# Every large on-chip tile moved to a multiple of 128 bytes (a two-block transformer in float32, one core)

## The chip, the cores and the metric

One core of one Trainium2 chip runs the whole program. The metric is the device time of one execution in microseconds; a figure for a kernel is the median of its runs. TensorE is PE in the profile (its weight loads are PEld), VectorE is DVE, ScalarE is ACT, GpSimd is POOL, and SP issues most of the DMAs.

## The reference

512 tokens of 1024 features pass two blocks in float32.

```python
def reference(x, mem, ...):
    x = x + hybrid_mixer(rms_norm(x))          # stick-breaking attention, gMLP, short conv; 3 gated branches; w_out
    x = x + memory_cross_attention(rms_norm(x), mem)   # 256 memory tokens: wk, wq, wv, wo
    x = x + swiglu(rms_norm(x))                # hidden 2816
    x = rms_norm(x, final_g)
    x = x + _mixer(_rms(x))                    # forget-gate attention, mLSTM, HGRN2; w_out_2
    x = x + _conv_glu(_rms(x))                 # hidden 2816, 3-tap causal conv on the up projection
    return x
```

## The kernel before

**Products.** Activations lie transposed, features on the 128 partitions and 512 tokens along the free axis, in 2 KiB slices. Every dense product is split: an operand is kept as a high part H, rounded to float32r, and a low part L, the rest, so one product is three matmuls (`mm3`, L361): H by H, L by H, H by L. 277 weight chunks of 128x1024 come from HBM one after the other into the ring `raw` (5 slots). ACT writes `WH` from it and DVE writes `WL` (L1465), each with 3 slots. PE uses chunks in the order of `PLAN`. The order on each engine is written out by hand, interleaved by fixed lists (`weave`), and all waits are semaphores that the author set; no tile framework adds any.

**Which operand is where.** In `tile` (L370) the weights are stationary (128 columns) and the activation slice moves (512 columns, 256 for the memory tokens). In `moving` (L382) and for wv of the cross attention the weights move and the activation is stationary. The activation pairs are:

- `XH`, `XL`: the normed input of a projection. Used by q, k, v, zv, zu, conv, the gates of the three branches, wq_xa, both ffn_up, and all input projections of the second block.
- `ZH`, `ZL`: branch outputs (288 matmuls), the input of w_out (192) and of wo_xa (192).
- `MH`, `ML`: the normed memory. Moving in wk_xa (8 tiles of 8 products), stationary in wv_xa.
- `HH1`, `HL1`, `HH2`, `HL2`: the hidden layers of the two feed-forward nets, for ffn_down1 and ffn_down2 (176 products each).
- `YYH`, `YYL`: the input of w_out2.

In the profile a matmul is named by its moving operand first: `pst<-HH,WL` moves `HH` against stationary `WL`. `HH` stands for both HH1 and HH2.

**Where the tiles lie.** A tile takes the same byte range in every partition. They are stacked in the order of the calls of `sb`, each start rounded up to 32 bytes, from byte 16512 (129 times 128) on. A closed stack gives its range back, so that `ZH`, `HH1`, `HH2`, `av1` and `YYH` all begin at the same byte, and q, k, kx, MH and so on lie over HH and HL. X, XH, XL, raw, WH, WL, cm and msk have sizes that are multiples of 128. Then come `col` (1168 bytes), `rcol` (16) and `gg` (32), after which every start is 96 past a multiple of 128, up to tiles behind other odd ones (`tmpb` 0 past, `pb` and `sg` 64 past).

Of the kernel before, what the change touches and what calls it, by code (L numbers as in the profile page):

```python
# [13 lines left out]
P = 128  # L14
T = 512
# [24 lines left out]
NCOLS = _n  # L40
# [109 lines left out]
def program(nc, xT, memT, wst, cols, rows, wsp, cmat, cmask, outT):  # L150
    es = ExitStack()
    with es:
        def sb(name, shape, dt=F32, stack=es):
            return stack.enter_context(nc.sbuf_tensor(name, shape, dt))
# [7 lines left out]
        raw = sb("raw", [P, NRAW, CH * P])  # L162
        WH = sb("WH", [P, NHL, CH * P], F32R)
        WL = sb("WL", [P, NHL, CH * P], F32R)
        cm = sb("cm", [P, 5, P])
        ones, upper, ident, halves, norms = (cm[:, i, :] for i in range(5))
        msk = sb("msk", [P, 8, P], U8)
        col = sb("col", [P, NCOLS])
        rcol = sb("rcol", [P, 4])
        gg = sb("gg", [P, 8])  # L170
        misc = sb("misc", [P, 6, T])
        acc = sb("acc", [P, 2, T])
        r_bc = misc[:, 0, :]
        rr = r12 = misc[:, 1, :]
        sq = [misc[:, 1, :], misc[:, 2, :]]
# [9 lines left out]
        st = ExitStack()  # L185
# [3 lines left out]
        row3 = sb("row3", [P, 3, T], stack=st)  # L189
        wT = sb("wT", [P, 4, P], stack=st)  # L190
        u, vz = X[:, 0:4, :], X[:, 4:8, :]
        ypad = sb("ypad", [P, T + 2], stack=st)
        tmpb = sb("tmpb", [P, 2, T], stack=st)
        st8 = sb("st8", [P, 16], stack=st)
        pb = sb("pb", [P, 2, 2, T], stack=st)
        sg_ = sb("sg", [P, 2, 2, T], stack=st)
        st.close()
        kx = sb("kx", [P, 8, MEM], stack=st)
        vx = sb("vx", [P, 2, D], stack=st)
        qx = sb("qx", [P, 8, T], stack=st)  # L200
        s8 = sb("s8", [P, 4, 8], stack=st)
        mrb = sb("mrb", [P, 4, MEM], stack=st)
        mraw = qx[:, 0:4, :].rearrange("p a (b t) -> p (a b) t", t=MEM)
        MH = sb("MH", [P, 8, MEM], F32R, st)
        ML = sb("ML", [P, 8, MEM], F32R, st)
        S2 = sb("S2", [P, 4, 2, MEM], stack=st)
        PT = [misc[:, 4:6, :], misc[:, 2:4, :], acc[:, :, :], mrb[:, :, :].rearrange("p (a b) t -> p a (b t)", b=2)]
        st.close()
        sty.close()
# [125 lines left out]
        def pe_program():  # L335
# [12 lines left out]
            def chunk(name):  # L348
# [3 lines left out]
                pe.wait_ge(wl, i + 1)  # L352
                return WH[:, i % NHL, :], WL[:, i % NHL, :]

            def units(w):
                return w.rearrange("p (u c) -> p u c", c=P)

            def mm(out, lhs, rhs, start=True, stop=True):
                return nc.tensor.matmul(out, lhs, rhs, start=start, stop=stop)  # L359
# [227 lines left out]
            def cross(s):  # L587
                b0, S = 4 + s, S2[:, s]
                for i in range(2):
                    free(b0)  # L590
                    pe.wait_ge(qx_ok, 2 * s + 2)
                    pe.wait_ge(kx_ok, 8)
                    for e in range(2):
                        for dd in range(2):
                            tb = (2 * i + e) * P
                            ins = mm(ps[b0][:, e * MEM:(e + 1) * MEM], qx[:, 2 * s + dd, tb:tb + P], kx[:, 2 * s + dd, :], dd == 0, dd == 1)
                    ins.then_inc(x_pe[s], 1)
                    yield
                    hold[b0] = (x_act[s], 3 * i + 2)
                    yield  # L600
                    yield
                    pe.wait_ge(x_dve[s], 5 * i + 5)
                    free(b0)
                    for si in range(2):
                        for e in range(2):
                            o = (2 * si + e) * P
                            ins = nc.tensor.transpose(ps[b0][:, o:o + P], S[:, e, si * P:(si + 1) * P], ident)
                    ins.then_inc(x_pe[s], 1)
                    yield
                    hold[b0] = (x_act[s], 3 * i + 3)  # L610
                pe.wait_ge(vx_ok, 2 * (s // 2) + 2)
                for dd in range(2):
                    b = b0 if dd == 0 else 2
                    free(b)
                    pe.wait_ge(x_act[s], 6)
                    for si in range(2):
                        ins = mm(ps[b][:, :], vx[:, si, s * 256 + dd * P:s * 256 + (dd + 1) * P], PT[s][:, si, :], si == 0, si == 1)
                    ins.then_inc(x_pe[s], 1)
                    yield
                hold[b0] = (zl_ok, 8 + 2 * s + 1)  # L620
                hold[2] = (zl_ok, 8 + 2 * s + 2)
                yield
# [230 lines left out]
            for m, b in enumerate(w_out2):  # L853
                i = PLAN.index(("w_out2", m))
                h, l = units(WH[:, i % NHL, :]), units(WL[:, i % NHL, :])
                for x, k in enumerate(YY_ORDER[6:]):
# [10 lines left out]
        def act_program():  # L867
# [3 lines left out]
            def run(func, out, in_, **kw):  # L871
                return nc.scalar.activation(out, in_, func, **kw)  # L872
# [229 lines left out]
            def cross(s):  # L1102
                b0, S, m_ = 4 + s, S2[:, s], s8[:, s]
                pv = ps[b0][:, :].rearrange("p (e s) -> p e s", s=MEM)
                for i in range(2):
                    yield
                    table(LNEXP)
                    act.wait_ge(x_dve[s], 5 * i + 2)
                    if i:
                        act.wait_ge(x_pe[s], 2)  # L1110
                    for e in range(2):
                        run(ACT.Exp, S[:, e, :], pv[:, e, :], bias=m_[:, e:e + 1], accum_out=m_[:, 2 + e:3 + e]).then_inc(x_act[s], 1)
                    yield
                    yield
                    yield
                    act.wait_ge(x_pe[s], 2 * i + 2)
                    run(ACT.Copy, PT[s][:, :, i * 256:(i + 1) * 256], ps[b0][:, :].rearrange("p (a t) -> p a t", t=256)).then_inc(x_act[s], 1)
                yield
                yield
                act.wait_ge(mm_, DONE["w_out", 7])  # L1120
                for dd in range(2):
                    act.wait_ge(x_pe[s], 5 + dd)
                    run(ACT.Copy, ZH[:, 2 * s + dd, :], ps[b0 if dd == 0 else 2][:, :]).then_inc(zh_ok, 1)
                yield
# [323 lines left out]
        def dve_program():  # L1448
# [12 lines left out]
            def split():  # L1461
                i = at["split"]
                at["split"] += 1
                dve.wait_ge(wh, i + 1)
                vec.tensor_tensor(WL[:, i % NHL, :], raw[:, i % NRAW, :], WH[:, i % NHL, :].bitcast(F32), ALU.subtract).then_inc(wl, 1)  # L1465

# [242 lines left out]
            def cross(s):  # L1709
                S, m_ = S2[:, s], s8[:, s]  # L1710
                pv = ps[4 + s][:, :].rearrange("p (e s) -> p e s", s=MEM)
                for i in range(2):
                    yield
                    dve.wait_ge(x_pe[s], 2 * i + 1)
                    vec.tensor_reduce(m_[:, 0:2], pv, AX.X, ALU.max).then_inc(x_dve[s], 1)
                    dve.wait_ge(x_dve[s], 5 * i + 1)
                    vec.tensor_scalar(m_[:, 0:2], m_[:, 0:2], -1.0, None, ALU.mult).then_inc(x_dve[s], 1)
                    yield
                    dve.wait_ge(x_act[s], 3 * i + 2)
                    vec.reciprocal(m_[:, 4:6], m_[:, 2:4]).then_inc(x_dve[s], 1)  # L1720
                    dve.wait_ge(x_dve[s], 5 * i + 3)
                    for e in range(2):
                        vec.tensor_scalar(S[:, e, :], S[:, e, :], m_[:, 4 + e:5 + e], None, ALU.mult).then_inc(x_dve[s], 1)
                    yield
                    yield
                yield
                yield
                for dd in range(2):
                    dve.wait_ge(zh_ok, 8 + 2 * s + dd + 1)
                    lo(ZL[:, 2 * s + dd, :], ps[4 + s if dd == 0 else 2][:, :], ZH[:, 2 * s + dd, :]).then_inc(zl_ok, 1)  # L1730
                yield
# [736 lines left out]
```

## Time and profile before

| | |
|---|---|
| median of 3 runs | 1736.02 us (1735.88 to 1737.95) |
| the profiled execution, its own time | 1737.55 us |
| its span, first to last instruction | 1735.8 us |
| mean granted TensorE clock | 0.994 |
| PE, PEld busy | 1692.5 us (98%), 1343.8 us (77%) |
| DVE, ACT, POOL busy | 896.8 us (52%), 657.7 us (38%), 163.3 us (9%) |
| DMA | 164.28 MB, 95 GB/s on average |

The durations that the profile gives matmuls overlap, since they are pipelined: a 128x512 matmul of 0.39 us starts some 0.23 us after the one before. The pace of PE is therefore read from starts: last start less first start, over the number of starts between them. The granted clock of 1.00 is TensorE's higher level (2.4 GHz), 0.5 the lower one (1.2 GHz).

### The profile page before, as it was taken

What the parts mean: (1) busy time and instruction counts of PE and PEld (TensorE: products, weight loads), DVE (VectorE), ACT (ScalarE), POOL (GpSimd) and SP (SyncE); (2) the same over time, 40 slices, a digit from 0 to 9 for tenths busy, and PEclk for the clock granted to TensorE, in tenths of its full rate; (3) what the DMA queues carried; (4) which work ended last, traced back from release to release, by engine and by line L of the source; (5) the groups of instructions that cost most, each with busy time, mean ns of one, the idle gap of its engine ahead of it and who ended that gap; (6) DMA issues with size and microseconds to landing.
All of it is one profiled execution on the core that took longest, in us unless ns stands there. A gap on an engine that the chain in (4) does not pass through costs nothing.

```text
span 1735.8 us, 19182 instructions
## 1 busy us (share of the span) xinstructions
PE 1692.5 (98%) x7824; PEld 1343.8 (77%) x7824; DVE 896.8 (52%) x1184; ACT 657.7 (38%) x935; POOL 163.3 (9%) x170
## 2 busy tenths in 40 slices
PE   7999999999999899999999999999999999999999
PEld 6777777778788668888888887777765888888887
DVE  4336664455463444444443326967545577777321
ACT  4244333333442433222222325246565444444211
POOL 2000100111110002000000111322111200000000
PEclk9999999999999999999999999999999999999999
DMA  6222222222433222223233223321212322323321
GB/s 241 85 86 73 73 73 85 78 93 97 158 101 105 73 86 94 96 97 97 97 97 103 87 91 103 132 99 62 61 37 91 102 98 96 97 95 97 103 92 54
DMA packets 47303, 164.28 MB, mean 95 GB/s; under 512 B 5024, under 2 KB 5152, under 8 KB 46896
## 3 DMA queue, kind: packets, MB, share of 16 engines
q1 hardware_dynamic: 46032, 158.88, 27.5%
q0 software_dynamic: 896, 3.70, 0.7%
q8 instruction: 62, 1.02, 0.2%
q10 hardware_dynamic: 288, 0.48, 0.1%
q14 instruction: 25, 0.20, 0.0%
HBM read 158.81 MB, written 4.23 MB: 94 GB/s over the span
## 4 chain that ended last, share of the span: by engine, by line
PE 90%; DVE 4%; ACT 3%; issue 2%; DMA 1%; POOL 0%; SPq 0%; ACTq 0%; DVEq 0%; POOLq 0%
PE pst L359 89%; ACT WH L872 1%; ACT L877 1%; PE pst L519 0%; PE pst L753 0%; DVE WL L1465 0%; DMA raw<-wst 0%; DMA X<-xT 0%; DVE qx L1684 0%; ACT ZH L872 0%; DVE XL L1477 0%; DVE ZL L1473 0%; DVE scr L2044 0%; ACT misc L872 0%; ACT Sx L872 0%
## 5 line engine op out<-in xcount | busy, mean ns | idle before, releaser
L359 PE MATMUL pst<-XH,WH 128*128 128x512 f32 x1320 | 528.0, 400 | 1.6 <-ACT v L872 1.6
L1465 DVE TENSOR_TENSOR WL<-raw,WH 128x1024 fp32r<-128x1024 f32 x277 | 345.5, 1248 | 346.0 <-ACT WH L872 345.9
L359 PE MATMUL pst<-XH,WL 128*128 128x512 f32 x1320 | 515.3, 390 | 0.0
L359 PE MATMUL pst<-XL,WH 128*128 128x512 f32 x1320 | 515.2, 390 | 0.0
L872 ACT ACTIVATE WH<-raw 128x1024 fp32r<-128x1024 f32 x277 | 291.4, 1052 | 391.6 <-PE pst L359 387.0
L359 PEld LDWEIGHTS pst<-XH,WH 128*128 128x128 f32 x1320 | 248.4, 188 | 66.2 <-issue 13.9
L359 PEld LDWEIGHTS pst<-XH,WL 128*128 128x128 f32 x1320 | 248.3, 188 | 52.8
L359 PEld LDWEIGHTS pst<-XL,WH 128*128 128x128 f32 x1320 | 248.6, 188 | 52.1 <-issue 2.9
L359 PE MATMUL pst<-HH,WH 128*128 128x512 f32 x352 | 139.2, 396 | 0.0
L359 PE MATMUL pst<-HL,WH 128*128 128x512 f32 x352 | 139.2, 396 | 0.0
L359 PE MATMUL pst<-HH,WL 128*128 128x512 f32 x352 | 139.2, 396 | 0.0
L2165 POOL TENSOR_TENSOR acc<-acc,misc 128x512 f32<-128x512 f32 x42 | 70.8, 1686 | 601.3 <-ACT misc L872 599.7
L872 ACT ACTIVATE misc<-misc 128x512 f32<-128x512 f32 x86 | 54.2, 631 | 141.1 <-DVE misc L1768 65.9
L359 PE MATMUL pst<-ZH,WH 128*128 128x512 f32 x224 | 91.0, 406 | 0.0
L359 PE MATMUL pst<-ZH,WL 128*128 128x512 f32 x224 | 88.6, 396 | 0.0
L359 PE MATMUL pst<-ZL,WH 128*128 128x512 f32 x224 | 88.5, 395 | 0.0
L2128 DVE SCALAR_TENSOR_TENSOR misc<-gp,col,misc 128x512 f32<-128x512 f32 x88 | 66.2, 752 | 27.9 <-ACT misc L872 26.4
L359 PEld LDWEIGHTS pst<-HH,WH 128*128 128x128 f32 x352 | 66.1, 188 | 16.0
L359 PEld LDWEIGHTS pst<-HL,WH 128*128 128x128 f32 x352 | 66.1, 188 | 16.0
L359 PEld LDWEIGHTS pst<-HH,WL 128*128 128x128 f32 x352 | 66.1, 188 | 15.9
L872 ACT ACTIVATE HH<-misc 128x512 fp32r<-128x512 f32 x44 | 27.8, 633 | 131.7 <-DVE misc L1773 98.9
L872 ACT ACTIVATE misc<-gp,col 128x512 f32<-128x512 f32 x44 | 35.9, 816 | 84.6 <-DVE gp L2150 84.6
(249 smaller groups left out, 1861.7 us busy)
## 6 DMA issues: line engine op xcount, KB each, us to landing
raw<-wst SPq DMA_DIRECT2D x277, 512.0 KB, 3.7
X<-xT SPq DMA_DIRECT2D x8, 512.0 KB, 7.5
xs<-X SPq DMA_DIRECT2D x1, 2048.0 KB, 8.7
nC<-cd POOLq DMA_DIRECT2D x4, 512.0 KB, 8.5
X<-xs SPq DMA_DIRECT2D x2, 1024.0 KB, 5.5
outT<-X SPq DMA_DIRECT2D x8, 256.0 KB, 4.3
qx<-memT SPq DMA_DIRECT2D x1, 1024.0 KB, 4.8
gt<-cd POOLq DMA_DIRECT2D x1, 1024.0 KB, 4.6
```

The source lines that it names most:

```text
L359: return nc.tensor.matmul(out, lhs, rhs, start=start, stop=stop)
L872: return nc.scalar.activation(out, in_, func, **kw)
L877: nc.scalar.preload_act_table_set(name)
L1465: vec.tensor_tensor(WL[:, i % NHL, :], raw[:, i % NRAW, :], WH[:, i % NHL, :].bitcast(F32), ALU.subtract).then_inc(wl, 1)
L2128: vec.scalar_tensor_tensor(o, gp[:, e, j:T + j], col[:, a:a + 1], o, ALU.mult, ALU.add).then_inc(hs, 1)
L2165: gp.tensor_tensor(acc[:, which, :], acc[:, which, :], sq[j % 2], ALU.add).then_inc(acp, 1)
```

## The change

The same instructions stand in the same order on every engine, with the same waits; only addresses differ. `misc` and `acc` are declared before the odd small tensors. `col`, `rcol` and `gg` become columns of one tensor of 2560 bytes. `ypad`, `st8` and `s8` go behind the large tiles of their stage.

```diff
@@ -162,14 +162,13 @@
         WL = sb("WL", [P, NHL, CH * P], F32R)
+        misc = sb("misc", [P, 6, T])
+        acc = sb("acc", [P, 2, T])
         cm = sb("cm", [P, 5, P])
         ones, upper, ident, halves, norms = (cm[:, i, :] for i in range(5))
         msk = sb("msk", [P, 8, P], U8)
-        col = sb("col", [P, NCOLS])
-        rcol = sb("rcol", [P, 4])
-        gg = sb("gg", [P, 8])
-        misc = sb("misc", [P, 6, T])
-        acc = sb("acc", [P, 2, T])
+        cols_ = sb("colsb", [P, 640])
+        col, rcol, gg = cols_[:, 0:NCOLS], cols_[:, NCOLS:NCOLS + 4], cols_[:, NCOLS + 4:NCOLS + 12]
@@ -189,21 +188,21 @@
-        ypad = sb("ypad", [P, T + 2], stack=st)
         tmpb = sb("tmpb", [P, 2, T], stack=st)
-        st8 = sb("st8", [P, 16], stack=st)
         pb = sb("pb", [P, 2, 2, T], stack=st)
         sg_ = sb("sg", [P, 2, 2, T], stack=st)
+        ypad = sb("ypad", [P, T + 2], stack=st)
+        st8 = sb("st8", [P, 16], stack=st)
...
-        s8 = sb("s8", [P, 4, 8], stack=st)
         mrb = sb("mrb", [P, 4, MEM], stack=st)
...
         S2 = sb("S2", [P, 4, 2, MEM], stack=st)
+        s8 = sb("s8", [P, 4, 8], stack=st)
```

First byte of some tiles, and what it is past a multiple of 128:

| tile | before | | after | |
|---|---|---|---|---|
| X, XH, XL | 16512, 32896, 49280 | 0 | the same | 0 |
| raw, WH, WL | 65664, 86144, 98432 | 0 | the same | 0 |
| misc, acc | 115552, 127840 | 96 | 110720, 123008 | 0 |
| cm | 110720 | 0 | 127104 | 0 |
| ZH, HH, YYH | 131936 | 96 | 133248 | 0 |
| ZL, YYL | 148320 | 96 | 149632 | 0 |
| HL | 176992 | 96 | 178304 | 0 |
| Sx | 156512 | 96 | 157824 | 0 |
| tmpb | 199552 | 0 | 198784 | 0 |
| MH, ML | 201696, 209888 | 96 | 202880, 211072 | 0 |
| gp | 222048 | 96 | 223360 | 0 |

## Rows read from the trace of the kernel before

**Rows 1.** The page, parts 2 and 4.
```profile
PEclk9999999999999999999999999999999999999999
...
PE 90%; DVE 4%; ACT 3%; issue 2%; DMA 1%; POOL 0%; SPq 0%; ACTq 0%; DVEq 0%; POOLq 0%
```

**Rows 2.** The chain in order of time: start us, us, engine, line, count.
```profile
627.35 411.98 PE pst L359 x1786
```

**Rows 3.** Tile XH, 700:900: ns min/median/max, first and last start.
```profile
L359 PE MATMUL pst<-XH,WH x295: 389/389/389, 699.7 to 899.6; 128*128 128x512 f32 x148
```

**Rows 4.** Tile HH, 920:1030, same columns.
```profile
L359 PE MATMUL pst<-HH,WL x158: 395/396/396, 919.9 to 1029.8; 128*128 128x512 f32 x158
```

**Rows 5.** Tiles XH, then ZH, 370:442, same columns.
```profile
L359 PE MATMUL pst<-XH,WH x65: 389/389/395, 370.3 to 436.8; 128*128 128x512 f32 x65
...
L359 PE MATMUL pst<-ZH,WL x38: 395/396/397, 371.4 to 441.5; 128*128 128x512 f32 x38
```

**Rows 6.** Timeline of PE, 20:21.5, then 611:613.6: start us, us, line.
```profile
19.62 0.39 PE L359 MATMUL pst<-WH,XH 128*128 128x512 f32 x1
...
21.43 0.39 PE L359 MATMUL pst<-WH,XL 128*128 128x512 f32 x1
...
610.98 0.39 PE L359 MATMUL pst<-WL,MH 128*128 128x512 f32 x1
...
613.55 0.39 PE L359 MATMUL pst<-WH,MH 128*128 128x512 f32 x1
```

**Rows 7.** Timeline of PE, 515:516.5.
```profile
514.92 0.28 PE L359 MATMUL pst<-MH,WL 128*128 128x256 f32 x1
...
516.48 0.29 PE L359 MATMUL pst<-MH,WH 128*128 128x256 f32 x1
```

**Rows 8.** Groups by form, PE: xcount | busy us, mean ns | idle us before.
```profile
L359 PE MATMUL pst<-HH,WH 128*128 128x512 f32 x352 | 139.2, 396 | 0.0
...
L359 PE MATMUL pst<-ZH,WH 128*128 128x512 f32 x224 | 91.0, 406 | 0.0
...
L359 PE MATMUL pst<-YYH,WH 128*128 128x512 f32 x64 | 27.3, 427 | 0.5 <-DVE YYL L1473 0.5
...
L359 PE MATMUL pst<-MH,WH 128*128 128x256 f32 x64 | 20.0, 313 | 3.8 <-DVE ML L1473 3.8
...
L359 PE MATMUL pst<-WH,MH 128*128 128x512 f32 x32 | 13.2, 413 | 0.0
```

**Rows 9.** Stages: us, then PE, PEld, DVE, ACT, POOL busy; granted clock, DMA share, GB/s.
```profile
445.00:500.00 55.00, 49.77 (x222) 40.03 (x220) 32.20 (x43) 26.83 (x46) 12.37 (x8) 1.00 0.40 143
500.00:527.00 27.00, 26.22 (x183) 25.35 (x184) 11.12 (x10) 11.95 (x18) 0.44 (x1) 0.88 0.46 153
```

**Rows 10.** The chain, 444:501.
```profile
456.70 20.46 PE pst L359 x88
```

**Rows 11.** Tile tmpb, whole span, then tile misc, 700:900.
```profile
L1609 DVE TENSOR_TENSOR tmpb<-tmpb,misc x4: 691/692/692, 159.2 to 219.9; 128x512 f32<-128x512 f32 x4
L872 ACT ACTIVATE ZH<-tmpb x4: 614/630/632, 160.4 to 220.6; 128x512 fp32r<-128x512 f32 x4
...
L872 ACT ACTIVATE HH<-misc x19: 632/632/633, 700.0 to 895.8; 128x512 fp32r<-128x512 f32 x19
...
L1773 DVE TENSOR_TENSOR misc<-misc x18: 691/691/692, 710.2 to 895.1; 128x512 f32<-128x512 f32 x18
```

**Rows 12.** Tile Sx, 1195:1240.
```profile
L359 PE MATMUL pst<-Sx,av x56: 271/275/377, 1200.0 to 1234.0; 128*128 128x128 f32 x56
...
L753 PE MATMUL pst<-cm,Sx x28: 270/272/328, 1197.5 to 1229.4; 128*128 128x128 f32 x28
```

**Rows 13.** Timeline, 900:903: a chunk is split beside steady matmuls.
```profile
900.99 0.39 PE L359 MATMUL pst<-XH,WH 128*128 128x512 f32 x1
...
901.09 1.04 ACT L872 ACTIVATE WH<-raw 128x1024 fp32r<-128x1024 f32 x1
...
902.35 0.39 PE L359 MATMUL pst<-XH,WH 128*128 128x512 f32 x1
```

## Prediction

> **What bounds the kernel now.** I read the chain that ended last first: PE holds 90% of it, DVE 4% and ACT 3%, and the granted clock is at its higher level nearly everywhere [rows 1]. In order of time one piece of that chain is 412 us of PE alone, 1786 matmuls without a wait on anything [rows 2]. So in most of the span the time is the number of matmuls times PE's pace, and whatever changes the pace changes the time one for one. The change touches no instruction, only addresses; the first question is whether the trace of before already holds both kinds of address at one kind of work.
>
> It does. In ffn_up1 the moving operand is XH or XL, 0 past a multiple of 128 bytes. The three matmuls of a product alternate, so 295 of one kind are 294 x 3 = 882 starts, in 899.6 - 699.7 = 199.9 us: 226.6 ns a matmul [rows 3]. In ffn_down1 the moving operand is HH or HL, 96 past, against the same weight slots WH and WL: 157 x 3 = 471 starts in 109.9 us, 233.3 ns [rows 4]. The size is the same 128x512. The step is 6.7 ns, which at 2.4 GHz is 16 columns, or 64 bytes of float32 in a partition. One duration differs by the same step: median 389 ns with XH, 396 with HH.
>
> Could the stage make this difference and not the tile? From 370 to 442 us the third branch alternates tiles of both kinds, in the same surroundings: XH 389 ns, ZH 396 [rows 5]. ZH is 96 past too. The stationary operand counts as well: when WH and WL move (aligned in both cases) against XH, 8 starts take 1.81 us, 226 ns; against MH, 96 past, 11 starts take 2.57 us, 234 ns [rows 6]. So one odd operand of the two is enough. I read from all four that a matmul of this type costs one step of 16 columns more when an operand straddles one more 64-byte piece than it must. Every odd operand in the list of groups is 32 past a multiple of 64, so the rows can't say whether 64 or 128 is the unit; the new addresses meet both.
>
> **The change part by part.** After it both operands of every one of these matmuls lie where XH, WH and WL lie now, 0 past. XH even has the same place in 2048 bytes (128 past) that ZH, HH, MH and YYH get. What is bought is 6.7 ns for each matmul that had an odd operand and that PE doesn't wait ahead of. Counts are three times the rows of the groups [rows 8]:
>
> - ffn_down1 and ffn_down2, HH and HL: 1056. Both are steady stretches of PE. 1056 x 6.7 = 7.1 us.
> - wo_xa, ZH and ZL: 192, in the steady piece that begins at 627 us: 1.3 us.
> - the three branches, ZH and ZL: 288. PE leads there too: 1.9 us.
> - w_out, ZH and ZL: 192. From 445 to 500 us PE is idle for 5 of 55 us and the chain hops between ACT, DVE and the memory norm [rows 9]; it is PE's for one piece of 88 matmuls [rows 10]. I take these 88: 0.6 us. Bounds 0 and 1.3.
> - wk_xa, MH and ML moving with 256 columns: 192. The odd pace at the higher clock is 13 starts in 1.56 us, 120 ns [rows 7]; no aligned one of this size is in the trace. The bounds are 0, if some other limit holds at this size, and 6.7. In time that is 0 to 1.3 us. I take 6.7 ns each, since the only seen cause of the step doesn't scale with the columns: it costs the same for a stationary operand of 128 columns as for a moving one of 512. Between 500 and 527 us the mean clock is 0.88 [rows 9], so some 30 of them run at the lower level, which I leave out. 162 x 6.7 = 1.1 us.
> - wv_xa, MH and ML stationary: 96, mostly on the chain: 0.6 us, bounds 0.3 and 0.6.
> - w_out2, YYH and YYL: 192, the first of them behind waits for YYL. 1.2 us, bounds 0.9 and 1.3.
>
> Sum: 7.1 + 1.3 + 1.9 + 0.6 + 1.1 + 0.6 + 1.2 = 13.8 us. All low bounds give 11.5, all high ones 14.8.
>
> DVE and ACT I cost at nothing, and not because they are hidden. ACT reads tmpb, aligned now, in a median of 630 ns, and misc, 96 past, in 632; DVE adds two tiles with tmpb in 692 and with misc alone in 691 [rows 11]. At most 2 ns of 630 on their 7% of the chain (some 120 us) is 0.4 us. The plain float32 products and transposes are few: with Sx and av, both odd, the duration is 275 ns, with cm (aligned) moving 272 [rows 12]. 3 ns on the some 400 small ones would be 1.2 us; as they stand in the stages where PE is not alone on the chain, I take 0 and keep 1.2 for the range. DMAs into raw, the bulk of the traffic, go to the same bytes as before.
>
> Nothing new is late: a chunk feeds 24 matmuls, 5.6 us at the old pace of ffn_down and 5.4 at the new, which ffn_up already runs at with the same ring and more work on DVE and ACT beside it, without an idle PE [rows 2].
>
> The profiled execution took 1737.55 us of its own time around a span of 1735.8, so 1737.55 - 13.8 = 1723.8. It stands 1.5 above the median of the runs; the same sum from the median is 1736.0 - 13.8 = 1722.2.
>
> **The rule that speaks against it.** ACT and DVE above show no effect of 32 bytes, and their rows alone would make the change worth nothing; PE's rows show 6.7 ns. The Trainium skill (SBUF — State Buffer, "Door 1: The DMA port swizzle") says that the memory has lines of 16 bytes and that only the crossing from line to line costs. 96 and 0 past 128 are both multiples of 16, so by that rule the layout is indifferent for every engine and the time stays 1736. DVE and ACT agree with it here, PE's two paces (226.6 and 233.3) don't, unless something else makes them.
>
> **Rivals.**
>
> - *The pace goes with the place and not with the alignment: no change.* Every slow activation tile (Z, H, YY, M) begins at byte 131936 or above, every fast one ends at or below 110720. If far bytes were slow for PE's reads, the same matmuls stay at 233.3 and the time is 1736 (1734.5 to 1737.5). For it: the trace has no float32r operand that is aligned and high, or odd and low. Against it: HH begins at 131936 and HL at 176992, 45056 bytes apart, and both have the mean of 396 ns [rows 8]; an effect of distance would hardly come in one step of exactly 16 columns. The rule on lines ends in the same place. 8%.
> - *Slower, because everything now shares one phase.* Today the reads and writes of DVE and ACT on misc are 96 past while PE reads at 0 past; after the change they all run at 0. If accesses of equal phase disturbed each other, PE would take a step more now and then. Price: one step of 6.7 ns each; the gain of 13.8 us is gone when 2060 matmuls take one. There are 277 chunks of 24, less 96 because wv_xa's 8 chunks feed 12 each, 6552 in all, of which 2208 are in my list; if all the 4344 others did, it were 29.1 us against 13.8, that is 1751.3. Against it: ACT and DVE split raw into WH and WL at 0 past, beside PE reading XH and WH at 0 past, and six starts around such a split take 902.35 - 900.99 = 1.36 us, 227 ns each [rows 13]. 3%.
> - *The gain is real but half of it comes back as waits.* If the stretches outside the two ffn_down and wo_xa were paced by hand-offs and not by PE, only 7.1 + 1.3 = 8.4 us stay: 1727.6. For it: in the 55 us of w_out the chain hops between engines [rows 9, 10]. Against it: in the stretch of the third branch the durations with XH and ZH are bare of waits [rows 5], and the projections of the second block all use XH, already aligned, and are not in my sum. An added stretch at the lower clock, 3.4 us long, would cost 1.7 us. 5%.
>
> **How the numbers follow.** The forecast, that the step of 16 columns goes away everywhere, gets 84%: 1722.2, its own range 1719.5 (all high bounds, the small products, some luck with the waits) to 1725. The single time is its. The overall range reaches a little on, to a part of the third rival and below for a larger share of the small products: 1718.5 to 1727.5. Outside it are the no-change case, the slower one and half of the third rival. A measurement of this kernel tells about 0.2%, 3.5 us, from no change. Forecast and third rival are both faster by more: 89%. Within 0.2%: 8% from the first rival. Slower: 3%.
>
> **What would show it.** In the profile of the changed kernel the matmuls with HH, HL, ZH, ZL, YYH and YYL should have a median of 389 ns in steady stretches and start every 226.7 ns; wv_xa's likewise. wk_xa's pace should be 113 ns if my reading of that size holds, 120 if not. ACT and DVE groups should keep their means within 3 ns, and PE with XH should stay at 389 in ffn_up; 396 there would mean the second rival. If HH stays at 396 the place decides and not the alignment. The prediction is wrong if the pace falls as said and the span doesn't: then the chain has to show new pieces of ACT, DVE or DMA between 450 and 625 us and around 1310.

## The result, and the profile after

| | before | after |
|---|---|---|
| median, us | 1736.29 (4 runs, 1735.88 to 1737.95) | 1727.13 (4 runs, 1726.16 to 1727.53) |
| ratio | | 0.9945, 95% interval 0.9927 to 0.9962 |
| profiled execution, us | 1737.55 | 1727.28 |
| its span, us | 1735.8 | 1725.5 |
| mean granted clock | 0.994 | 0.993 |
| PE, DVE, ACT, POOL busy, us | 1692.5, 896.8, 657.7, 163.3 | 1682.3, 902.8, 657.6, 159.7 |

The changed kernel is 9.2 us faster by the medians and 10.3 by the spans of the profiled executions. 13.8 was forecast. The time, 1727.1, is inside the overall range (1718.5 to 1727.5) by 0.4 us, but outside the forecast's own, which ended at 1725. Faster holds, and a quarter of the gain is missing by the spans, a third by the medians. The medians of this document leave out one execution, of the kernel with 64 bytes ahead of everything: it took 5827.1 us at a granted clock of 0.284.

On the page of the changed kernel PE holds 90% of the chain as before [rows 1], and the group of HH has a mean of 389 ns in place of 396 [rows 8].

Tile HH of the changed kernel, 920 to 1030 us, then tile XH, 700 to 900 us (ns min/median/max, first and last start, as in [rows 3, 4]):

```profile
L358 PE MATMUL pst<-HH,WL x162: 389/389/389, 919.9 to 1029.3; 128*128 128x512 f32 x162
```

```profile
L358 PE MATMUL pst<-XH,WH x295: 389/389/389, 699.8 to 899.7; 128*128 128x512 f32 x148
```

161 x 3 = 483 starts of HH in 109.4 us are 226.5 ns; XH stands at 199.9 / 882 = 226.6, as before. The rows give starts to 0.1 us, which leaves some 0.2 ns of doubt: both are the pace that XH had before.

DVE and ACT didn't move. Tile misc, 700 to 900 us, now aligned, against [rows 11]:

```profile
L1772 DVE TENSOR_TENSOR misc<-misc x18: 691/692/693, 707.5 to 892.5; 128x512 f32<-128x512 f32 x18
L871 ACT ACTIVATE HH<-misc x18: 632/633/633, 708.2 to 893.2; 128x512 fp32r<-128x512 f32 x18
```

Where the time went is read from the chain in order of time, at places that both kernels have. Pieces of the kernel before that [rows 2, 10] don't hold (start us, us, engine, line, count):

```profile
10.69 36.83 PE pst L359 x154
...
199.34 19.80 PE pst L359 x88
...
443.38 0.64 ACT ZH L872
...
477.25 0.69 DVE X L1669
...
500.78 47.71 PE pst L359 x277
548.51 0.69 DVE qx L1703
...
1313.31 19.85 PE pst L359 x64
...
1336.61 396.04 PE pst L359 x1724
1732.67 0.69 DVE X L1747
```

The same of the changed kernel:

```profile
10.48 37.59 PE pst L358 x154
...
199.90 19.93 PE pst L358 x88
...
442.28 0.64 ACT ZH L871
...
455.49 21.86 PE pst L358 x88
477.44 0.69 DVE X L1668
...
500.88 46.78 PE pst L358 x277
547.68 0.69 DVE qx L1702
...
625.94 407.20 PE pst L358 x1786
...
1307.15 20.11 PE pst L358 x64
...
1330.72 391.66 PE pst L358 x1724
1722.40 0.69 DVE X L1746
```

The start of a piece before less its start after is the time saved up to there. The differences between neighbours are what each section gave:

| section, by the chain | forecast, us | got, us |
|---|---|---|
| start to 199 us (float32r matmuls only on tiles that were aligned) | 0 | -0.56 |
| to 443, the three branches | 1.9 | 1.66 |
| to 477, first part of w_out | 0.6 | -1.29 |
| to 549, rest of w_out, wk_xa, wq_xa | 1.1 | 1.02 |
| to 627, wv_xa and its surroundings | 0.6 | 0.58 |
| to 1313, wo_xa, ffn_up1, ffn_down1, heads | 4.8 | 4.75 |
| to 1337, first part of w_out2 | 0.3 | -0.27 |
| to the end, rest of w_out2, ffn_up2, ffn_down2 | 4.4 | 4.38 |
| sum | 13.7 | 10.27 |

(627.35 stands in [rows 2].) The steady sections gave what was forecast, to 0.1 us. The largest loss is the piece of 88 matmuls of w_out: 20.46 us before [rows 10], it takes 21.86 after, though every matmul in it is of the faster kind.

The forecasts are the prediction's terms cut at the same places: each ffn_down 528 x 6.7 = 3.5, and 0.9 of w_out2 in the last section. At the start the first piece of 154 took 37.59 us for 36.83, though the addresses of its operands did not change. The timeline of PE has the reason, first of the kernel before, then of the changed one:

```profile
15.06 0.39 PE L359 MATMUL pst<-WL,XH 128*128 128x512 f32 x1
```

```profile
16.54 0.40 PE L358 MATMUL pst<-WH,XL 128*128 128x512 f32 x1
```

These are the first matmuls at the faster pace. The ones ahead of them start some 427 ns apart, 10 from 10.69 us on before and 14 from 10.48 on after. Four more at 427 in place of 227 ns are 0.8 us. (The column of the granted clock has 1.00 for 10 to 15 us in both traces; the starts say otherwise.) So PE came up to the higher level later in this execution; nothing in the edit is known to cause it, and the kernel with two pads below has the same, up to 16 us.

The windows of the changed kernel name the cause in w_out and in what follows (columns as in [rows 9]):

```profile
445.00:460.00 15.00, 12.68 (x50) 9.90 (x49) 7.65 (x10) 7.02 (x12) 1.84 (x1) 0.89 0.83 311
500.00:527.00 27.00, 26.12 (x187) 25.11 (x188) 11.76 (x10) 12.00 (x19) 0.54 (x1) 0.92 0.47 157
```

From 445 to 500 us the granted clock was 1.00 before [rows 9]; now it is 0.89 from 445 to 460. A mean of 0.89 over 15 us is 3.3 us at the lower level. There a matmul starts every 426.7 ns (see w_out2 below) and not every 226.7, so such a stretch costs PE 47% of its length, 1.6 us. Without it the piece is 21.86 - 1.6 = 20.3: 0.2 less than before. Of its 88 matmuls 73 in the trace of before move Z, and 73 steps of 6.7 ns would be 0.5.

The 1.02 us of the section that ends at 549 us are not wk_xa's pace either. Tile MH of the changed kernel, 510 to 522 us, and then wv_xa, where it is stationary, 505 to 626 us:

```profile
L358 PE MATMUL pst<-MH,WL x34: 283/283/283, 509.8 to 521.7; 128*128 128x256 f32 x34
```

```profile
L358 PE MATMUL pst<-WH,MH x32: 389/389/580, 581.1 to 618.5; 128*128 128x512 f32 x32
```

33 x 3 = 99 starts in 11.9 us are 120 ns, the pace before [rows 7]. With 256 columns this change of layout is worth nothing. What the section got is again the clock: from 500 to 527 us it is 0.92 against 0.88 [rows 9], so that (1 - 0.92) x 27 = 2.2 us of PE's work are lost there against 3.2. Before 500 us PE waits for the memory norm, and the part of the lower-clock stretch that lies there costs less. wv_xa did fall to 389 ns.

In w_out2 a third thing is seen. Timeline of PE in the kernel before, two starts in w_out2 at the lower level:

```profile
1314.56 0.63 PE L359 MATMUL pst<-YYL,WH 128*128 128x512 f32 x1
...
1318.40 0.62 PE L359 MATMUL pst<-YYL,WH 128*128 128x512 f32 x1
```

The changed kernel has the same two from 1308.41 to 1312.25. Both times 9 starts in 3.84 us, 426.7 ns a matmul, with the old address and with the new one. That is 512 columns at 1.2 GHz and not one more. At the lower level the step doesn't exist. The Trainium skill (TensorE: Matmul & The Clock Gate, "Wait — 56ns, not 53.3ns?") states just this for the lower level, N columns divided by 1.2 GHz, and for the higher one N / 2.4 GHz plus some 2.5 ns, by which 512 columns are an estimated 215.8 ns. The trace agrees with the first and not with the second, since these matmuls start every 226.7 ns at best.

How much of this first piece lies at the lower level differs too (the windows of the two pieces, before and after):

```profile
1313.31:1333.16 19.85, 19.85 (x65) 12.45 (x65) 8.12 (x13) 5.90 (x11) 1.11 (x3) 0.86 0.28 106
```

```profile
1307.15:1327.26 20.11, 20.11 (x65) 12.57 (x65) 8.13 (x13) 5.90 (x11) 1.11 (x3) 0.84 0.27 105
```

(1 - 0.86) x 19.85 = 2.8 us of the clock are lost before and (1 - 0.84) x 20.11 = 3.2 after. These 0.4, less some 30 steps at the higher level (0.2), are about the 0.27 by which the piece is longer.

### The profile page after: what moved, and what is told of

The parts are those of the page before. It is cut to its first block, busy times and chain, and to the rows that moved or that the text cites. A ratio compares the mean times of both kernels' runs of the same rounds, so it can differ in the third digit from the quotient of the medians.

```text
span 1725.5 us, 19182 instructions
## 1 busy us (share of the span) xinstructions
PE 1682.3 (97%) x7824; PEld 1344.7 (78%) x7824; DVE 902.8 (52%) x1184; ACT 657.6 (38%) x935; POOL 159.7 (9%) x170
## 3 DMA queue, kind: packets, MB, share of 16 engines
q8 instruction: 62, 1.02, 0.3%
## 4 chain that ended last, share of the span: by engine, by line
PE 90%; DVE 4%; ACT 3%; issue 2%; DMA 1%; POOL 0%; SPq 0%; ACTq 0%; DVEq 0%; POOLq 0%
PE pst L358 89%; ACT WH L871 1%; ACT L876 1%; PE pst L518 0%; PE pst L752 0%; DVE WL L1464 0%; DVE qx L1683 0%; DMA X<-xT 0%; DMA raw<-wst 0%; ACT ZH L871 0%; DVE ZL L1472 0%; DVE scr L2043 0%; ACT misc L871 0%; ACT Sx L871 0%; POOL acc L2164 0%
## 5 line engine op out<-in xcount | busy, mean ns | idle before, releaser
L358 PEld LDWEIGHTS pst<-XH,WH 128*128 128x128 f32 x1320 | 248.7, 188 | 65.9 <-issue 13.8
L2127 DVE SCALAR_TENSOR_TENSOR misc<-gp,colsb,misc 128x512 f32<-128x512 f32 x88 | 66.2, 752 | 27.9 <-ACT misc L871 26.3
L358 PEld LDWEIGHTS pst<-HH,WH 128*128 128x128 f32 x352 | 66.1, 188 | 13.8
L358 PEld LDWEIGHTS pst<-HL,WH 128*128 128x128 f32 x352 | 66.1, 188 | 13.7
L871 ACT ACTIVATE misc<-gp,colsb 128x512 f32<-128x512 f32 x44 | 35.9, 816 | 84.6 <-DVE gp L2149 84.6
```

What stands on the lines that cost most here:

```text
L2127: vec.scalar_tensor_tensor(o, gp[:, e, j:T + j], col[:, a:a + 1], o, ALU.mult, ALU.add).then_inc(hs, 1)
```

## The experiments

The reading of the prediction was that the address of an operand decides the pace. The runs test it against the distance between the two operands. In the pads below, `sb("pad", [P, 8])` is an unused tile of 8 x 4 = 32 bytes that moves all tiles declared after it. "Distance" is the first byte of the activation tile less that of WH, modulo 256. WL lies 48 x 256 behind WH, X and its pairs whole multiples of 256 ahead of it. Before, the distance of Z, H and YY was 224 and of M 96; after, all are 0.

**One pad ahead of everything: the absolute place.** The changed kernel, all distances kept:

```diff
+        sb("pad", [P, 16])    # 64 bytes; [P, 8]: 32; [P, 96]: 384
         X = sb("X", [P, 8, T])
```

> The changed kernel with one unused tile of 64 bytes ahead of X, so that every large tile lies 64 past a multiple of 128; nothing else differs. If 64 bytes is the unit (my reading of the step of 16 columns), the pace of every 128x512 float32r matmul stays 226.7 ns, durations 389, and the time is that of the changed kernel, 1727 (1724 to 1730). If the unit is 128, each of the 6552 matmuls has an odd operand: 233.3 ns, 1727 + 6552 x 6.7 = 1771.

Median of 3 runs 1726.6 us, ratio to the kernel before 0.9936 (95% interval 0.9920 to 0.9953; ratios below likewise). No row of this one's trace is read (see the result). By the time alone nothing is lost at 64 past.

> The changed kernel with 32 unused bytes ahead of X: every large tile 32 past a multiple of 128, both operands of every matmul alike. One odd operand is enough and a second one costs nothing more: pace 233.3 ns, 1727 + 6552 x 6.7 ns = 1771. Each odd operand costs its own step: 240 ns, 1814. What counts is the difference between the two operands and not the address itself: 226.7 ns and 1727. DVE and ACT groups keep their means in any case.

Median 1726.6, ratio 0.9933 (0.9917 to 0.9950), span 1725.3. Tile HH, 920 to 1030 us:

```profile
L359 PE MATMUL pst<-HH,WL x162: 389/389/389, 920.0 to 1029.4; 128*128 128x512 f32 x162
```

All operands of all matmuls lie 32 past a multiple of 64, HH among them, and 483 starts take 109.4 us: 226.5 ns, 389 each. So the reading in the prediction, that a matmul pays when an operand straddles a 64-byte piece too many, is wrong. What is kept here is only where the operands lie to each other. DVE and ACT keep 691 and 632 ns on tile misc here too, 32 past (700 to 900 us).

> The changed kernel with 384 unused bytes ahead of X, which puts every large tile and every slice of it on a multiple of 512. The aligned pace of 226.7 ns is 34 steps of 16 columns for a tile of 32. If the two more come from crossing some larger block at the place 128 past, a start on 512 would save one or both: 220 ns for 6552 matmuls, 1727 - 44 = 1683. If they belong to the instruction, the pace and the time stay at 226.7 ns and 1727 (1724 to 1730); this I hold the likelier.

Median 1726.6, ratio 0.9939 (0.9925 to 0.9954), span 1724.8, HH again at 389 ns. The 32 columns beyond 512 in 226.7 ns (544 at 2.4 GHz) stay at every place that was tried.

> As the last one, but with every large tile and slice on a multiple of 2048 bytes (msk and an unused tile of 896 bytes stand ahead of X, the tensor of small columns has 384 columns). A moving slice of 2 KiB then crosses no boundary of 1024 or 2048 inside. Block theory: 213 to 220 ns and 1640 to 1683. Fixed cost of the instruction: 226.7 ns, 1727 (1724 to 1730). If equal phase in 2048 bytes disturbs (all operands at 0), slower than that, the XH groups above 389 ns.

Median 1727.1, ratio 0.9943 (0.9928 to 0.9958), span 1725.5, HH at 389. Equal phase in more bits neither helps nor disturbs.

**Only the activations away from the weights: the distance.**

```diff
+        sb("pad", [P, 8])     # 32 bytes; [P, 16]: 64
         ZH = sb("ZH", [P, 8, T], F32R, sty)
```

> The changed kernel with 32 unused bytes ahead of ZH: ZH, HH, YYH, MH and all that is declared behind them lie 32 past a multiple of 128; X, XH, XL, raw, WH, WL, misc, acc stay at 0. With all tiles 32 past the pace was the aligned one, so my first theory (the address of an operand itself) has fallen. New theory, distance: a matmul costs one step of 16 columns more when its moving and its stationary operand differ in their place in 64 bytes. Then H, Z, Y and wv_xa go back to 233.3 ns and the time to 1736 to 1738. Rival, neither: what changed in before was misc, acc and the small tensors; then the pace stays 226.7 ns and 1727.

Median of 10 runs 1737.3, ratio 0.9999 (0.9987 to 1.0011): the whole gain is gone, while X and its pairs, the weights, misc and acc stay where the changed kernel has them. Tile HH, 920 to 1030 us:

```profile
L359 PE MATMUL pst<-HH,WL x157: 393/396/397, 920.2 to 1029.4; 128*128 128x512 f32 x157
```

156 x 3 = 468 starts in 109.2 us, 233.3 ns. Together with the 32-byte pad ahead of everything this is the decisive pair: HH begins at byte 133280 in both, and the pace is 226.5 in one and 233.3 in the other.

> The same with 64 unused bytes ahead of ZH: moving and stationary operand differ by 64 past a multiple of 128 in the 2208 matmuls. Distance with a unit of 64: no step, 226.7 ns, 1727 (1724 to 1730). Distance with a unit of 128: a step, 233.3 ns, 1736 to 1738.

Median 1730.0, ratio 0.9961 (0.9946 to 0.9976), span 1729.9. Tile HH, 920 to 1030 us:

```profile
L359 PE MATMUL pst<-HH,WL x161: 392/392/392, 919.7 to 1029.6; 128*128 128x512 f32 x161
L359 PE MATMUL pst<-HH,WH x161: 394/394/394, 919.9 to 1029.8; 128*128 128x512 f32 x161
```

480 starts in 109.9 us, 229.0 ns: a third of a step on average. The three matmuls of a product now differ, 394 and 392 ns, and 388 with HL. Neither 64 nor 128 as a plain unit gives this.

The matmuls of 256 columns are not indifferent after all. Tile MH of this run, 512 to 524 us:

```profile
L359 PE MATMUL pst<-MH,WH x35: 280/280/280, 511.8 to 523.8; 128*128 128x256 f32 x35
```

34 x 3 = 102 starts in 12.0 us are 117.6 ns, 2 ns less than at a distance of 0 or 96. So at this size a distance of 64 is better than 0.

**Only the weights away from the activations.** The first moves both weight rings by 32 bytes, the second WL alone; the second pad brings what follows back to a multiple of 128. It doesn't bring it back to the old distance: Z, H, YY and M lie 96 from WH in the first, and 128 from WH and 96 from WL in the second.

```diff
+        sb("pad", [P, 8])                 # in the second: behind WH
         WH = sb("WH", [P, NHL, CH * P], F32R)
         WL = sb("WL", [P, NHL, CH * P], F32R)
+        sb("pad2", [P, 24])
```

> The changed kernel with WH and WL 32 bytes further (32 past), all other large tiles at 0. Distance theory: all 6552 float32r matmuls have operands 32 apart, 233.3 ns, those with XH too: 1727 + 6552 x 6.7 ns less what is hidden around w_out and the heads, 1765 to 1771. If only activations beside the far bytes count, 1727. ACT writing WH from raw and DVE reading both, 32 apart then, should keep their means (1052 and 1249 ns).

One execution, 1759.1 us, span 1757.3, 31.8 more than the changed kernel's and short of the 1765 expected. Tile XH, 700 to 900 us, and the chain's pieces (changed kernel: 407.20 from 625.94, 20.11 from 1307.15, 391.66 from 1330.72):

```profile
L360 PE MATMUL pst<-XH,WL x286: 395/396/396, 699.9 to 899.4; 128*128 128x512 f32 x143
```

```profile
634.88 418.95 PE pst L360 x1786
...
1328.79 18.92 PE pst L360 x64
...
1351.16 403.03 PE pst L360 x1724
```

285 x 3 = 855 starts in 199.5 us are 233.3 ns: XH, the fast tile of every kernel so far, pays 6.7 ns once the weights lie elsewhere. The piece of 1786 costs 11.75 more (1786 x 6.7 ns = 12.0), that of 1724 11.37 (11.6). The some 3040 others would be 20 us more and give 8.7. Ahead of the first piece it is 8.94 us, between it and w_out2 0.95 (274.96 against 274.01), and w_out2's first 64 even take 1.19 less: the granted clock is 0.91 in them for 0.84 in the changed kernel. What else hides the rest wasn't taken apart.

> WL alone 32 past; WH, XH, ZH, HH, raw at 0. In a product the order is (moving XH, stationary WH), (XL, WH), (XH, WL). If the step is paid by the matmul whose own two operands differ, it is the third: XH,WL goes from 389 to 395 ns, XL,WH stays. If it comes from the weight load of the next matmul, which reads while this one streams, it is the second, XL,WH, whose neighbour loads WL. A third of 6552 pays in both cases: 2184 x 6.7 = 14.6 us, 1739 to 1742.

One execution, 1757.5 us, span 1755.7. Tile XH and tile XL, 700 to 900 us; and the timeline at 800 us:

```profile
L360 PE MATMUL pst<-XH,WL x286: 389/389/389, 700.0 to 899.5; 128*128 128x512 f32 x143
...
L360 PE MATMUL pst<-XH,WH x286: 395/395/395, 700.2 to 899.7; 128*128 128x512 f32 x143
```

```profile
L360 PE MATMUL pst<-XL,WH x287: 400/400/400, 699.7 to 899.9; 128*128 128x512 f32 x144
```

```profile
799.85 0.40 PE L360 MATMUL pst<-XL,WH 128*128 128x512 f32 x1
799.85 0.19 PEld L360 LDWEIGHTS pst<-XH,WL 128*128 128x128 f32 x1
```

The price of one odd ring out of two is that of both: again 855 starts in 199.5 us, and 418.92 us for the chain's piece of 1786. For the products with X only one matmul in three has an operand at an odd distance, XH with WL, and that one keeps 389 ns. XL with WH pays, 400 ns, and XH with WH 395. Start to start it is the same order: on average over these 200 us the next matmul follows XL,WH after 239.5 ns, XH,WH after 232.2 and XH,WL after 228.3 (226.2 to 227.0 in the changed kernel). In the timeline the load for XH with WL starts at 799.85, together with the matmul of XL: the matmul that pays most is the one that streams while the odd weights are being loaded, the second of the expectation's two cases. Its size, a third of all, is wrong (part of the miss is the distance of 128 to the high tiles, which pays, see below; but X alone pays in full). And XH with WH pays 6 ns although neither its own weights nor the ones loaded beside it are odd; that is not explained.

The Trainium skill (SBUF — State Buffer, "Who interferes with whom") has two independent read ports for TensorE, one for the moving operand and one for weight loads, and says that PE never waits on anyone. These rows don't agree to the last per cent: with its own two operands where they were and only the weights loaded beside it elsewhere, a matmul takes 11 ns of 389 more.

**A scan of the distance.** Two kernels, one execution each. Tiles of the changed kernel are allotted 512 bytes larger and begun some bytes into the allotment: HH1, HL1 at 16 and HH2, HL2 at 4 bytes with Z at 128, then 128, 256 and 192.

```diff
+        def off(name, k, o, stack):
+            t = sb(name, [P, k * T + 128], F32R, stack)
+            return t[:, o:o + k * T].rearrange("p (k t) -> p k t", t=T)
...
+        ZH, ZL = off("ZH", 8, 32, sty), off("ZL", 8, 32, sty)    # second: 48
...
-            HHs.append(sb(f"HH{which}", [P, HID, T], F32R, st))
+            HHs.append(off(f"HH{which}", HID, (4, 1)[which - 1], st))   # second: (32, 64)
```

> The changed kernel with three groups of activations at other places in 128 bytes, WH and WL at 0: ZH, ZL 128 bytes further (a multiple of 128 but not of 512), HH1, HL1 16 bytes further, HH2, HL2 4 bytes further. At a distance of 32 the pace was 233.3 ns, at 64 a mean of 228.9. Theory of distance in 128 bytes: Z stays at 226.7 in wo_xa; H at 16 and 4 bytes pays a step (233.3 ns) in both feed-forward nets, since any distance that is no multiple of the unit straddles. Rival, lines of 16 bytes: 16 is free (226.7), 4 pays, and as much or more than 32 did. Total with all of H paying: 1727 + 1056 x 6.7 ns = 1734.

1736.4 us, span 1734.6, above the 1734 expected. Tile HH at 16 bytes (ffn_down1), then at 4 (ffn_down2):

```profile
L361 PE MATMUL pst<-HH,WL x159: 390/392/398, 920.0 to 1029.8; 128*128 128x512 f32 x159
```

```profile
L361 PE MATMUL pst<-HH,WL x141: 397/401/403, 1609.7 to 1709.6; 128*128 128x512 f32 x141
```

474 starts in 109.8 us are 231.6 ns, 420 in 99.9 are 237.9. Even 4 bytes pay, and more than 32. Z at 128, in wo_xa, has 48 x 3 = 144 starts from 640.0 to 673.5 us, 232.6 ns.

> The same with ZH, ZL at 192, HH1, HL1 at 128 and HH2, HL2 at 256 bytes. A unit of 128: H at 226.7 ns in both nets, Z as at 64 (229). A unit of 256 or 512: ffn_down1 slower than 226.7, and for 512 ffn_down2 too. Some distance may also be better than 0, as single matmuls were at 64 (HL moving 226.0 against 226.7): then below 226.7. Total 1727 to 1730.

1728.7 us, span 1727.0. Tile HH at 128 (ffn_down1), at 256 (ffn_down2), and tile ZH at 192 (wo_xa):

```profile
L361 PE MATMUL pst<-HH,WL x158: 392/395/399, 919.9 to 1029.8; 128*128 128x512 f32 x158
```

```profile
L361 PE MATMUL pst<-HH,WL x148: 388/390/390, 1609.9 to 1709.8; 128*128 128x512 f32 x148
```

```profile
L361 PE MATMUL pst<-ZH,WL x46: 393/394/395, 639.8 to 671.3; 128*128 128x512 f32 x46
```

471 starts in 109.9 us: 233.3 ns at 128. 441 in 99.9: 226.5 at 256. 135 in 31.5: 233.3 at 192. A multiple of 128 is not enough, a multiple of 256 is. That the change's 128-byte rule gave 256 everywhere is luck of the tiles' sizes. (96 in the table is tile HH of the kernel with both rings moved: 381 starts in 89.0 us.)

| distance, bytes | 0, 256 | 4 | 16 | 32 | 64 | 96 | 128 | 192 | 224 |
|---|---|---|---|---|---|---|---|---|---|
| ns a matmul of 512 columns | 226.5 | 237.9 | 231.6 | 233.3 | 229.0 | 233.6 | 233.3 | 233.3 | 233.3 |

**The least edit.** The kernel before with one or two unused tiles:

```diff
         gg = sb("gg", [P, 8])
+        sb("pad", [P, 8])
         misc = sb("misc", [P, 6, T])
...
+        sb("pad2", [P, 32], stack=st)     # only in the kernel with two pads
         MH = sb("MH", [P, 8, MEM], F32R, st)
```

> The kernel of before with one unused tile of 32 bytes behind gg and nothing moved otherwise: misc, acc, ZH, HH, MH, YYH then begin at a multiple of 128, ypad, st8, s8, col, rcol and gg stay where they were in the order, tmpb lies 32 past and pb 96 past. If the distance between the two operands of the float32r matmuls is all that the change was, the time is that of the changed kernel, 1727 (1724 to 1730). If the order of the small tiles or the alignment of tmpb, pb and sg has a part in it, it lies between 1727 and 1736.

Median 1723.2 (1722.8 to 1726.4), ratio 0.9923 (0.9907 to 0.9940), span 1721.4. Tile HH, 920 to 1030 us; MH stationary, 505 to 626 us; two pieces of the chain:

```profile
L360 PE MATMUL pst<-HH,WL x163: 388/390/390, 919.6 to 1029.8; 128*128 128x512 f32 x163
```

```profile
L360 PE MATMUL pst<-WH,MH x32: 391/396/580, 577.7 to 615.5; 128*128 128x512 f32 x32
```

```profile
198.84 18.36 PE pst L360 x88
...
453.05 20.26 PE pst L360 x88
```

HH: 486 starts in 110.2 us, 226.7 ns. M lies at distance 128 now, and wv_xa keeps 396 ns, which says once more that the unit is 256. The time is 4 us below the changed kernel's at the same pace. The pieces say where: 88 matmuls of the first branch take 18.36 us (19.93 in the changed kernel, the piece at 199.90), the 88 of w_out 20.26 (21.86), the 64 of w_out2 18.98 (20.11). The first two are 1.6 us each, the price of one stretch of 3.4 us at the lower clock: the granted clock is 1.00 from 199 to 203 us and through the piece of w_out. In w_out2's 64 it is 0.90 for 0.84.

> The kernel before with the 32-byte tile behind gg as in the run with one pad, and one more unused tile of 128 bytes ahead of MH, which makes the distance from MH and ML to WH and WL a multiple of 256 instead of an odd multiple of 128. If the distance in units of 256 bytes decides, wv_xa's 96 matmuls start every 226.7 ns instead of 233.3 and the duration with MH stationary falls from 396 to 389 ns; everything else stays. That is 0.6 us less than the 1723.2 of the kernel with one pad: 1722.6, with 1721.5 to 1724 for the usual scatter. If multiples of 128 were enough, wv_xa would not move. A second question is whether the small tensors behind MH or the tensor placement of the changed kernel make the 4 us between it (1727.1) and the kernel with one pad: if the lower-clock stretch near 440 us belongs to the changed kernel's placement of the branch tensors (ypad and st8 behind the others), it stays away here as well, and near 184 us too; if it falls by chance of each build, it may be back, and the time is 1724 to 1727.

Median 1723.8 (1722.6 to 1727.0), ratio 0.9925 (0.9908 to 0.9941); the profiled execution had a span of 1725.2. MH stationary, 505 to 626 us, and the w_out piece:

```profile
L361 PE MATMUL pst<-WH,MH x32: 389/389/582, 580.9 to 618.3; 128*128 128x512 f32 x32
```

```profile
455.41 21.86 PE pst L361 x88
```

wv_xa is at 389 ns. And this execution has the lower-clock stretch in w_out, to the hundredth of a microsecond as in the changed kernel, with the old order of the branch's tiles. So the stretch comes without the changed kernel's layout too. Single executions of one kernel fall on levels some 3.5 us apart: 1723.2, 1722.6 and 1724.4 against 1727.0 with two pads, 1723.1 against 1726.3 to 1727.1 with all tiles 32 past, 1733.4 against 1735.8 to 1737.5 for the kernel before. But the levels are not equally frequent: of the 8 executions with one or two pads 6 lie below 1725 us, of the 19 of the changed kernel and its four shifts as a whole only 2. Whether something of the layout makes the stretches likelier is open.

## Why the prediction was right, and where not

**The two paces, and that they go one for one into the time: right.** 226.7 for 233.3 ns in every steady piece, 4.75 and 4.38 us of 4.8 and 4.4.

**What decides the pace: wrong, with the right outcome.** The premise that failed is "a matmul of this type costs one step of 16 columns more when an operand straddles one more 64-byte piece than it must". The trace of before had aligned pairs, and pairs with one odd operand, and no pair that was odd alike; so alignment and distance read the same. With everything 32 past nobody pays; with the activations alone 32 past everybody does. The distance between what streams and the weights decides, and its unit is 256 bytes. Nor is one step the only size: 2, 5 and 11 ns at 64, 16 and 4 bytes. That the forecast came out is luck: the new addresses are a multiple of 256 apart as well as multiples of 128.

**The first rival, far bytes are slow, or 16-byte lines make the layout indifferent: no.** HH at 133248 runs at 226.5 ns, and a distance of 16 bytes costs 5 ns.

**The second, equal phase disturbs: no.** XH stays at 389 ns in the changed kernel, with 2048-byte phases too.

**The third, half the gain comes back: near in size (1727.6 against 1727.1), and not by hand-offs.** The missing 3.5 us by the spans are: 1.9 in w_out (1.6 of it a stretch at the lower clock, which the prediction named under this rival at 1.7), 0.6 at the start, where PE came up to the higher level after four matmuls more, 0.6 in w_out2, 0.2 in the branches, and 0.2 in sum elsewhere. Most of it is clock and not layout. So the single time was missed by 4.9 us of a forecast gain of 13.8, and the forecast's own range with it; what held the overall range was its allowance for this rival.

**wk_xa: the choice of 6.7 ns against 0 was wrong.** 120 ns before and after, the bound that the prediction named and didn't take. The 1.0 us that the section gave were paid by a clock stretch that moved, so that it looks right and isn't.

**w_out: 88 steps counted, 73 there.** In the chain's piece some 15 matmuls don't move Z. Apart from the clock it gave 0.2 us of the 0.6.

**w_out2: mis-sized, 0.6 for 1.2.** Its first matmuls run at the lower level, where the step doesn't exist; 12 of them are 0.1 us. Another 0.4 is that more of the first piece lies at the lower level than before (3.2 against 2.8 us lost), and not all of its 64 move YY (43 in the trace).

**DVE and ACT at nothing: right.** DVE takes 692 ns and ACT 633 on aligned tiles.

Open: why 4 and 64 bytes cost what they do, and why 64 helps at 256 columns; why a third of odd loads costs as much as all; where the 32 columns beyond 512 come from. That TensorE's two reads disturb each other would fit the distance and the missing step at half clock, but it is argued, not shown. What places a lower-clock stretch in one execution and not in the next wasn't found.

## What to carry to other kernels

Where float32r matmuls of 512 columns run back to back, place the moving tile and the tile the weights are loaded from a multiple of 256 bytes apart; the absolute place is free, and 0, 32 or 96 past 128 is the same to what only DVE and ACT touch. Look for it as two paces of one shape in a trace, and move the whole stack once: one pad of 32 bytes gave the same pace as the reordering here, for all but wv_xa. Before a difference of 2 or 3 us is given to an edit, compare the same piece of the chain and the granted clock of its window in both traces.

## What the runs showed of the hardware

- A 128x512 float32r matmul starts every 226.7 ns at best at the higher clock, 544 columns' time, and every 426.7 at the lower one, exactly 512. One of 256 columns starts every 120 ns at distance 0, 288 columns' time. So 32 columns are lost at either size at the higher level, and none at the lower one at 512 columns.
- The distance between the moving tile and the weights adds 2 to 11 ns at 512 columns (4 to 224 bytes) and nothing at the lower clock (224). At 256 columns 96 bytes add nothing and 64 take 2 ns off.
- With one of two weight rings 32 bytes off, the matmul that streams while the odd weights are loaded takes 11 ns more and the next but one 6.
- A stretch of 3.4 us at the lower clock costs a steady stream of these matmuls 1.6 us (88 matmuls of w_out in 21.86 and 20.26 us).
